# An fp32 transformer block on one Trainium2 core: its MLP by one level of Strassen's scheme

## The chip, the cores and the metric

The program runs on one core of a Trainium2 chip. The metric is the device time of one execution in microseconds, lower is better. The core's engines are called PE (TensorE, the matmul engine; its weight loads are PEld), DVE (VectorE), ACT (ScalarE), POOL (GpSimd) and SP (SyncE, which here only starts transfers). Each runs its own list of instructions in order; they meet through semaphores.

## The reference, cut to what matters

```python
for l in range(DEPTH):                      # DEPTH = 1
    h = _rmsnorm(x, ln_mix_g[l])
    ...                                     # projections, sparse attention, HGRN2, short conv
    x = x + mixed @ w_out[l]
    h = _rmsnorm(x, ln_mlp_g[l])            # x: 1024 tokens x 1024
    x = x + jnp.square(jax.nn.relu(h @ w_mlp_up[l])) @ w_mlp_down[l]   # 1024x4096, 4096x1024
...                                         # then a second block: MLA attention and pooling branch
```

All arrays are fp32. The MLP is two matrix products of 1024 x 1024 x 4096 multiply-adds each.

## The kernel before

Everything is kept transposed: a tile is 128 features (partitions) by 1024 tokens, and an activation of 1024 features is eight tiles `j`. To keep fp32 accuracy on PE, each operand is split in a high part (rounded to the engine's fp32r format) and a low part (the rest), and each product is three matmuls: high by high, high by low, low by high. A matmul has a 128x128 weight block and 512 tokens (`HALF`).

Matmul work is cut in **units**. A unit `n` makes one tile of 128 output features by 1024 tokens in one of two PSUM pairs, `pair[n % 2]`: two token halves by `kt` input tiles by three matmuls, so 48 matmuls where `kt` is 8. SP loads the weights of unit `n` to `raw` when POOL has split unit `n - 2`. POOL splits them in `w_hi` (L636, a cast) and `w_lo` (L638, a subtraction of two SBUF operands). PE multiplies (`product`, L708; `product_first`, L726, which takes the input tiles one by one as they become ready). The reader of the result frees the PSUM pair.

The stretch in question has, in order:

- the out product, 8 units. DVE adds each result to `xB` (L1893), squares it for the mean of squares (L1903), and ACT and DVE make the high and low parts of `xB * ln_mlp` in `actB` (L1411, L1905). The sum of squares is kept in `mt[1]` (L1908);
- the MLP, 4 groups of 16 units. The first 8 units of a group make 8 tiles of the hidden layer: DVE takes relu and multiplies by the root-mean-square factor `rstd` (L1922), ACT squares (L1418), DVE makes high and low part in `actA` (L1925, L1927). The other 8 units multiply these 8 tiles by their share of `w_mlp_down`, and DVE adds each result to `xB` (L1893). After the first MLP unit PE makes the mean of squares (key `ss1`, L981) from which ACT makes `rstd`. During the last 8 units the parts of the new `xB` are made for the second block (L1426, L1941);
- the second block's input product `in2`, 19 units.

The order on each engine is that of its code. The loops that are written with `units` are loops of the hardware, not unrolled. PE's whole inner loop is these lines:

```python
for half in halves:
    cols = slice(half * HALF, (half + 1) * HALF)
    for k in range(kt):
        wk = slice(k * P, (k + 1) * P)
        for i, (w, x) in enumerate(((w_hi, hi(k)), (w_hi, lo(k)), (w_lo, hi(k)))):
            last = nc.tensor.matmul(pair[par][:, cols], w[:, par, wk], x[:, cols], ...)
```

## Time and profile before

| | |
|---|---|
| time, median of 3 runs | 2575.23 us (2573.36 to 2575.47) |
| the profiled execution: its time, and its span | 2574.69 us, 2572.9 us |
| mean granted PE clock | 0.979 |
| busy: PE, DVE, POOL, ACT | 2445.7, 1281.0, 803.9, 558.5 us |
| moved to and from memory | 206.65 MB, mean 80 GB/s |

The span is what the profiler saw between the first and the last instruction; the device time has 1.8 us more. Matmuls overlap in the pipeline: a record's duration (389 ns) is longer than the distance to the next (about 227 ns), and the distance is what counts. Rows give a start and a duration in us, the engine, the line of the kernel, the operation, the tile that it writes and those that it reads; brackets hold the idle time before it and what ended it.

### The profile page before, as it was taken

To read this page: it belongs to the slowest core of one execution; us is meant where nothing else is said; L and a number is where in the kernel's file an instruction comes from. 1 tells how busy PE (TensorE), PEld (TensorE's weight loads), DVE (VectorE), ACT (ScalarE), POOL (GpSimd) and SP (SyncE) were. 2 spreads that over 40 slices of the span, in tenths; PEclk is the share of its full clock that TensorE was granted. 3 is DMA by queue.
4 is the path that set the end of the run, shared out by engine and by line. 5 is a ranking of instruction groups with operands and counts; after the bars stand their busy time and mean duration, and the time that the engine had idled before them with its cause. 6 is when DMAs were issued, how large, how long until landed. Compare 5 with 4: busy or idle time off the path is not lost. (4 is left out here: it accounts for less than half of the span.)

```text
span 2572.9 us, 30451 instructions
## 1 busy us (share of the span) xinstructions
PE 2445.7 (95%) x11722; PEld 2022.7 (79%) x11722; DVE 1281.0 (50%) x1639; ACT 558.5 (22%) x686; POOL 803.9 (31%) x741
## 2 busy tenths in 40 slices
PE   6999999989999899999999999999999999789996
PEld 4688878877888789787888888888888877579974
DVE  3699999975546245446541231321335200534378
ACT  3310241022222255211100000000000102334423
POOL 1123323322222364334333333333333331300154
PEclk9999999989999899999999999999999999999998
DMA  3022224642222421443111111111112110221122
GB/s 140 25 90 98 98 79 134 242 142 83 90 107 74 131 66 42 147 139 115 49 49 49 48 44 47 49 49 49 49 49 61 65 49 21 104 76 50 46 69 95
DMA packets 80036, 206.65 MB, mean 80 GB/s; under 512 B 7040, under 2 KB 30600, under 8 KB 79048
## 3 DMA queue, kind: packets, MB, share of 16 engines
q1 hardware_dynamic: 59552, 129.85, 16.0%
q10 hardware_dynamic: 20392, 75.52, 8.4%
q8 instruction: 64, 1.05, 0.2%
q14 instruction: 28, 0.23, 0.0%
HBM read 156.31 MB, written 50.34 MB: 80 GB/s over the span
## 5 line engine op out<-in xcount | busy, mean ns | idle before, releaser
L708 PE MATMUL pair<-actA,w_hi 128*128 128x512 f32 x3040 | 941.5, 391 | 0.0
L708 PEld LDWEIGHTS pair<-actA,w_hi 128*128 128x128 f32 x3040 | 568.8, 188 | 121.1 <-issue 4.8
L708 PE MATMUL pair<-actA,w_lo 128*128 128x512 f32 x1520 | 591.7, 389 | 0.0
L634 POOL TENSOR_TENSOR pad<-pad 128x1 f32<-128x1 f32 x206 | 49.8, 242 | 1636.7 <-PE pair L708 1293.2
L708 PE MATMUL pair<-actB,w_hi 128*128 128x512 f32 x1568 | 484.0, 390 | 0.0
L638 POOL TENSOR_TENSOR w_lo<-raw,w_hi 128x1024 fp32r<-128x1024 f32 (+2 forms) x206 | 475.3, 2307 | 16.5
L708 PEld LDWEIGHTS pair<-actB,w_hi 128*128 128x128 f32 x1568 | 294.4, 188 | 62.2 <-issue 1.4
L708 PEld LDWEIGHTS pair<-actA,w_lo 128*128 128x128 f32 x1520 | 285.3, 188 | 59.6
L708 PE MATMUL pair<-actB,w_lo 128*128 128x512 f32 x784 | 305.0, 389 | 0.0
L636 POOL CAST w_hi<-raw 128x1024 fp32r<-128x1024 f32 (+2 forms) x206 | 204.3, 992 | 0.0
L1893 DVE TENSOR_TENSOR xB<-pair,xB 128x1024 f32 (+1 forms) x40 | 49.0, 1225 | 297.8 <-PE pair L708 273.8
L1643 DVE MAX8 top<-pen 128x8 f32<-128x384 f32 (+5 forms) x192 | 171.7, 894 | 6.4
L708 PEld LDWEIGHTS pair<-actB,w_lo 128*128 128x128 f32 x784 | 147.2, 188 | 30.6
L1645 DVE MATCH_REPLACE8 pen<-top,pen 128x384 f32<-128x384 f32 (+5 forms) x192 | 168.1, 875 | 0.0
L1418 ACT ACTIVATE mt<-mt 128x1024 f32<-128x1024 f32 x32 | 34.0, 1061 | 563.4 <-DVE mt L1922 563.4
L1149 ACT ACTIVATE stage<-pair 128x1024 f32<-128x1024 f32 x52 | 53.3, 1025 | 397.1 <-PE pair L708 358.5
L1922 DVE SCALAR_TENSOR_TENSOR mt<-pair,rstd 128x1024 f32<-128x1024 f32 x32 | 39.2, 1225 | 185.9 <-PE pair L708 176.6
L708 PE MATMUL pair<-ysp,w_hi 128*128 128x512 f32 x336 | 103.3, 389 | 0.0
L1068 PE MATMUL pair<-actB,w_hi 128*128 128x512 f32 x256 | 83.0, 406 | 10.5 <-DVE xB L2079 6.7
L1685 DVE COPY_PREDICATED hattn<-hmask,pair 128x1024 f32<-128x1024 int32 x32 | 43.4, 1357 | 91.4 <-PE pair L813 91.4
L1817 DVE CUSTOM_DVE_ANT_0 Pr<-pair,pslot 128x128 f32<-128x128 f32 (+7 forms) x64 | 48.3, 757 | 75.8 <-PE pair L896 59.5
L726 PE MATMUL pair<-actA,w_hi 128*128 128x512 f32 x192 | 63.9, 416 | 16.3 <-DVE actA L1573 16.3
(285 smaller groups left out, 3068.9 us busy)
## 6 DMA issues: line engine op xcount, KB each, us to landing
raw<-w_in SPq DMA_DIRECT2D x80, 512.0 KB, 3.5
raw<-w_mlp SPq DMA_DIRECT2D x64, 512.0 KB, 3.5
proj<-stage ACTq DMA_DIRECT2D x52, 512.0 KB, 2.6
gates<-proj ACTq DMA_DIRECT2D x24, 512.0 KB, 5.4
raw<-w_out SPq DMA_DIRECT2D x24, 512.0 KB, 3.6
cin<-proj ACTq DMA_DIRECT2D x4, 1536.0 KB, 12.0
raw<-w_up SPq DMA_DIRECT2D x24, 256.0 KB, 2.7
X<-xT SPq DMA_DIRECT2D x8, 512.0 KB, 8.7
```

The lines of the kernel that those rows point to most:

```text
L634: nc.gpsimd.tensor_tensor(pad[:, 0:1], pad[:, 1:2], pad[:, 1:2], ALU.add)
L636: nc.gpsimd.tensor_copy(w_hi[:, par, 0:w], raw[:, par, 0:w]).then_inc(w_hi_ok, 1)
L638: nc.gpsimd.tensor_tensor(w_lo[:, par, 0:w], raw[:, par, 0:w], w_hi[:, par, 0:w].bitcast(F32), ALU.subtract).then_inc(w_split, 1)
L708: last = nc.tensor.matmul(pair[par][:, cols], w[:, par, wk], x[:, cols], start=(k == 0 and i == 0), stop=(k == kt - 1 and i == 2))
L726: last = nc.tensor.matmul(pair[par][:, cols], w[:, par, wk], x[:, cols], start=(k == 0 and i == 0), stop=(k == kt - 1 and i == 2))
L1068: mm = nc.tensor.matmul(pair[par][:, 0:HALF], w[:, par, wk], x[:, cols], start=(k == 0 and i == 0), stop=(k == NT - 1 and i == 2))
L1149: nc.scalar.activation(dst, pair[par][:, :], func).then_inc(unit_out[par], 1)
L1643: V.max(top8[:, :], sc).then_inc(topk, 1)
L1645: V.match_replace(sc, top8[:, :], sc, PICKED).then_inc(topk, 1)
L1685: V.copy_predicated(hattn[:, :, :], hmask[:, lv:lv + 1, :].broadcast_to([P, NB, P]), mpair(key)[:, :].rearrange("p (a b) -> p a b", b=P)). ...
L1817: V.tensor_tensor_reduce(Pr[i % 4][:, 0:n], s_out(i)[:, 0:n], pslot[:, i % 3, 0:n], -float(HD) ** -0.5, 3.0e38, ALU.add, ALU.min, low4[:, ...
L1893: V.tensor_tensor(x, pair[par][:, :], x, ALU.add).then_inc(unit_out[par], 1)
```

## The change

Both products of the MLP are made by one level of Strassen's scheme in Winograd's form. Features and tokens are cut in halves, so that a product of 2x2 by 2x2 blocks takes 7 block products `P1` to `P7` in place of 8. Their operands are blocks or sums of blocks, and their results are added up to the four result blocks.

- **Steps.** There are 32 steps (`STEPS`) of 7 products. In steps 0 to 15 (up) a step makes two tiles of the hidden layer: each product has 4 input tiles, 512 tokens, 3 matmuls, so 12 matmuls in one bank. In steps 16 to 31 (down) a step makes a quarter of the output from 4 hidden tiles: each product has 2 halves of a PSUM pair by 2 input tiles by 3, again 12 matmuls. All is unrolled.
- **Weights.** SP loads 1 MB for a step in `wraw`, double buffered. POOL makes the four sums of weight blocks (`weight_sum`); ACT makes the high part of each of the 7 weight operands (`weight_hi`, 128x512) and POOL the low part (128x512), into slots `wsp`: 5 slots to step 16, then 8, and 4 for the last step. A slot is written again when the product that used it is done.
- **Activations, up.** In the out product, whose units now go in the order `OUT_ORDER` (weights likewise), DVE also makes four sums of blocks from `xB` times `ln_mlp` (`chunk_sums`), in place in `xB`, which is parked in memory (`x_d`) before. ACT squares `xB` (DVE did), scales it (`scale_h`) and makes the high parts of the sums (`sum_hi`); DVE makes the low ones (`sum_lo`), 16 of each, 128x512.
- **Results, up.** DVE reads a bank after each product (`event`): a copy after P1, P5, P6, a sum after P2, P7, P3, and relu and `rstd` after P4. P6, P7, P4 go on in the bank of P1, and P3 in that of P5 (`banks`), so that each may begin when the reading of the product before it in that bank is done (`BANK_NEED`). Then `relu`, ACT's square (`square_out`), and four sums of hidden blocks on DVE (`unit_sums`). The seven hidden blocks are parked in memory (`hid_d`, 1.75 MB a step).
- **Down.** The parked blocks come back 512 KB at a time to `staged` (56 loads), ACT and DVE split them in the ring `tring` (`split_hi`, `split_lo`, 56 of each, 128x1024). `event` adds 128x1024 results to quarters of `xB`.
- **First step.** It has the order P1, P2, P5, P6, P3, P7, P4; `ss1` comes after P3; DVE's and ACT's work on the last tile, on the sums and on the results of this step is written out by hand.
- **Last step and `in2`.** The parts of `xB` are made in the last step and after it (`final_hi`, `final_lo`), and the first `in2` unit takes its input tiles in another order.

Core of the diff:

```diff
+OUT_ORDER = [0, 4, 1, 5, 2, 6, 3, 7]
+STEPS = 2 * N_PAIR
+WEIGHT = {"P1": "A11", "P2": "A12", "P3": "S4", "P4": "A22", "P5": "S1", "P6": "S2", "P7": "S3"}
+RAW_BLOCK = {"A11": 0, "A12": 1, "A21": 2, "A22": 3}
+RUN = [(0, p) for p in ("P1", "P2", "P5", "P6", "P3", "P7", "P4")]
+RUN += [(st, p) for st in range(1, STEPS) for p in ("P1", "P5", "P6", "P2", "P7", "P3", "P4")]
+NO = {key: i for i, key in enumerate(RUN)}
+N_RUN = len(RUN)
...
+def banks(i):
+    st, p = RUN[i]
+    kind = {"P2": "b", "P5": "c", "P3": "c"}.get(p, "a")
+    first, second = 1 - st % 2, st % 2
+    if st < N_PAIR:
+        return {"a": [(first, 0)], "b": [(first, 1)], "c": [(2 + st % 2, 0)]}[kind]
+    return {"a": [(first, 0), (first, 1)], "b": [(second, 0), (second, 1)],
+            "c": [(2 + st % 2, 0), (2 + st % 2, 1)]}[kind]
...
+        wsp = [at(f"wsp{i}", kb, [P, 2, HALF], F32R)
+               for i, kb in enumerate((168, 172, 176, 180, 16, 195.5, 199.5, 203.5))]
+        wsum = {"S1": at("wsum_a", 188, [P, HALF]), "S2": at("wsum_b", 190, [P, HALF]), "S4": at("wsum_c", 20, [P, HALF])}
+        wsum["S3"] = wsum["S1"]
...
+            def load_pair(st):
+                if st == 0:
+                    sp.wait_ge(w_split, FIRST["in2"])
+                elif st == 1:
+                    sp.wait_ge(unit_mm, FIRST["in2"])
+                else:
+                    sp.wait_ge(wt_ok, 7 * (st - 1))
+                sp.dma_start(wraw[:, st % 2, :], t["w_pair"][st]).then_inc(pair_in[st % 2], 16)
...
+            for i, (st, p) in enumerate(RUN):
+                if p == "P1":
+                    pool.wait_ge(pair_in[st % 2], 16 * (st // 2 + 1))
+                if i + 1 < N_RUN and WEIGHT[RUN[i + 1][1]][0] == "S":
+                    weight_sum(i + 1)
+                pool.wait_ge(wt_hi, i + 1)
+                k = RAW_BLOCK.get(WEIGHT[p])
+                src = wraw[:, st % 2, k * HALF:(k + 1) * HALF] if k is not None else wsum[WEIGHT[p]][:, :]
+                dst = wsp[W_SLOT[i]]
+                nc.gpsimd.tensor_tensor(dst[:, 1, :], src, dst[:, 0, :].bitcast(F32), ALU.subtract).then_inc(wt_ok, 1)
+            pool.wait_ge(wt_ok, N_RUN)
...
+            def run(i):
+                st, p = RUN[i]
+                pe.wait_ge(wt_ok, i + 1)
+                if BANK_NEED[i]:
+                    pe.wait_ge(evicted, BANK_NEED[i])
+                w = wsp[W_SLOT[i]]
+                fresh = p in ("P1", "P2", "P5")
+                if st < N_PAIR:
+                    subs, ks = 1, 4
+                    x = bsp[:, PARK_OF[p]] if PARK_OF[p] < 3 else tsp[:, PARK_OF[p] - 3]
+                else:
+                    subs, ks = 2, 2
+                    j = 7 * ((st - N_PAIR) // 2) + SPLIT_OF[p]
+                    pe.wait_ge(t_ok, 16 + j + 1)
+                    x = tring[j % T_RING]
+                for sub in range(subs):
+                    a, half = banks(i)[sub]
+                    out = pair[a][:, half * HALF:(half + 1) * HALF]
+                    for k in range(ks):
+                        if st == 0 and p in ("P1", "P2", "P3"):
+                            pe.wait_ge(lo_ok, base + NT + 2 * k + (1 if p == "P1" else 2))
+                        elif st == 0:
+                            pe.wait_ge(t_ok, 4 * (PARK_OF[p] - 3) + k + 1)
+                        wk = slice((sub * ks + k) * P, (sub * ks + k + 1) * P)
+                        for m, (wp, xp) in enumerate(((0, 0), (0, 1), (1, 0))):
+                            mm = nc.tensor.matmul(out, w[:, wp, wk], x[:, xp, k, :],
+                                                  start=(fresh and k == 0 and m == 0), stop=(k == ks - 1 and m == 2),
+                                                  skip_group_check=True)
+                mm.then_inc(mul_done, 1)
...
+            def weight_hi(i):
+                st, p = RUN[i]
+                if W_BEFORE[i] >= 0:
+                    act.wait_ge(mul_done, W_BEFORE[i] + 1)
+                elif W_SLOT[i] == 4:
+                    act.wait_ge(unit_mm, FIRST["in2"])
+                elif W_SLOT[i] > 4:
+                    act.wait_ge(squared_ok, 4 * N_PAIR)
+                k = RAW_BLOCK.get(WEIGHT[p])
+                if k is None:
+                    order = [q for q in RUN[7 * st:7 * st + 7] if WEIGHT[q[1]][0] == "S"]
+                    act.wait_ge(summed, 4 * st + order.index((st, p)) + 1)
+                    src = wsum[WEIGHT[p]][:, :]
+                else:
+                    act.wait_ge(pair_in[st % 2], 16 * (st // 2 + 1))
+                    src = wraw[:, st % 2, k * HALF:(k + 1) * HALF]
+                nc.scalar.copy(wsp[W_SLOT[i]][:, 0, :], src).then_inc(wt_hi, 1)
...
+            def scale_h(m):
+                j = OUT_ORDER[m]
+                act.wait_ge(x_tile[j], 32)
+                act.wait_ge(ss_sq, m + 1)
+                act.wait_ge(lo_ok, base + NT + m + 1)
+                nc.scalar.activation(xB[:, j, :], xB[:, j, :], ACT.Copy, scale=SM("ln_mlp", j)).then_inc(h_ok, 1)
...
+            def square_out(i):
+                st, p = RUN[i]
+                if p == "P4":
+                    act.wait_ge(evicted, i + 1)
+                else:
+                    act.wait_ge(relu_ok, 3 * st + ("P2", "P7", "P3").index(p) + 1)
+                if st == 0:
+                    act.wait_ge(t_ok, 12)
+                else:
+                    if p == "P2":
+                        act.wait_ge(b11_out, 16 * st)
+                    elif p != "P3":
+                        act.wait_ge(b2_out, 16 * st)
+                    act.wait_ge(tsum_ok, 16 + 4 * (st - 1) + {"P2": 1, "P3": 2, "P7": 4, "P4": 4}[p])
+                nc.scalar.activation(hid[:, HID_OF[p], :], u_of[p][:, :], ACT.Square).then_inc(squared_ok, 1)
...
+            def t_sums(src, dst, done, order):
+                b11, b12, b21, b22 = src
+                for q in order:
+                    if q == 0:
+                        V.tensor_tensor(dst[0], b12, b11, ALU.subtract).then_inc(tsum_ok, 1)
+                    elif q == 2:
+                        dve.wait_ge(tsum_ok, done + 1)
+                        V.tensor_tensor(dst[2], b22, b12, ALU.subtract).then_inc(tsum_ok, 1)
+                    elif q == 1:
+                        dve.wait_ge(tsum_ok, done + 2)
+                        V.tensor_tensor(dst[1], b22, dst[0], ALU.subtract).then_inc(tsum_ok, 1)
+                    else:
+                        dve.wait_ge(tsum_ok, done + 3)
+                        V.tensor_tensor(dst[3], b21, dst[1], ALU.subtract).then_inc(tsum_ok, 1)
...
+            def event(i):
+                st, p = RUN[i]
+                dve.wait_ge(mul_done, i + 1)
+                src = psum_of(i)
+                if st >= N_PAIR:
+                    if st == N_PAIR and p == "P1":
+                        dve.wait_ge(x_in, 16 * (NT + 1))
+                    if st == N_PAIR + 1 and p == "P1":
+                        dve.wait_ge(x_in, 16 * (NT + 3))
+                    first = {"P2": "P1", "P7": "P5", "P3": "P6"}.get(p)
+                    if first:
+                        dve.wait_ge(evicted, NO[st, first] + 1)
+                    acc = quarter(xB, st, {"P1": "P2", "P5": "P7", "P6": "P3"}.get(p, p))
+                    V.tensor_tensor(acc, src.rearrange("p (s n) -> p s n", n=HALF), acc, ALU.add).then_inc(evicted, 1)
+                    return
+                u = u_of[{"P1": "P2", "P5": "P7", "P6": "P3"}.get(p, p)][:, :]
+                used = {"P1": 1, "P5": 2, "P6": 3, "P4": 4}.get(p)
+                if used and st:
+                    dve.wait_ge(squared_ok, 4 * (st - 1) + used)
+                if p in ("P1", "P5", "P6"):
+                    V.tensor_copy(u, src).then_inc(evicted, 1)
+                elif p == "P4":
+                    V.scalar_tensor_tensor(u, src, 0.0, rstd[:, 0:HALF], ALU.max, ALU.mult).then_inc(evicted, 1)
...
+            def unit_sums(u):
+                dve.wait_ge(squared_ok, 4 * u + 4)
+                if u:
+                    dve.wait_ge(tsum_out, 16 * u)
+                t_sums([hid[:, HID_OF[p], :] for p in ("P2", "P3", "P4", "P7")],
+                       [hsum[:, q, :] for q in range(4)], 16 + 4 * u, (0, 2, 1, 3))
...
+            for m in range(NT - 1):
+                take_out(m)
+                low_out(m)
+                add_square(m)
+                dve.wait_ge(h_ok, m + 1)
+                chunk_sums(m // 2, (2, 1, 3) if m % 2 else (0,))
+            take_out(NT - 1)
+            for k in range(2):
+                sum_lo(0, k)
+            low_out(NT - 1)
+            for k in range(2, 4):
+                sum_lo(0, k)
+            event(0)
+            for k in range(3):
+                sum_lo(1, k)
+            add_square(NT - 1)
+            dve.wait_ge(ss_sum, NT + 1)
+            event(1)
+            event(2)
+            dve.wait_ge(h_ok, NT)
+            chunk_sums(3, (2, 1, 3))
+            sum_lo(1, 3)
+            event(3)
+            for k in range(4):
+                sum_lo(2, k)
...
+            for i in range(7, N_RUN):
+                st, p = RUN[i]
+                event(i)
+                if st < N_PAIR and p in ("P2", "P7", "P3"):
+                    relu(i)
+                if p == "P1" and st <= N_PAIR:
+                    unit_sums(st - 1)
+                for j in range(N_SPLIT):
+                    if T_TURN[j] == i:
+                        split_lo(j)
+                if st == STEPS - 1 and p in ("P5", "P6", "P2", "P7"):
+                    final_lo(STEPS - 2, ("P2", "P7", "P3", "P4")[("P5", "P6", "P2", "P7").index(p)])
+                if st == STEPS - 1 and p in ("P7", "P3", "P4"):
+                    final_lo(st, {"P7": "P2", "P3": "P7", "P4": "P3"}[p])
+            final_lo(STEPS - 1, "P4")
             base += NT
```

## Rows read from the trace of the kernel before

**Rows 1.** The page: busy time, share of the span and instructions of each engine.
```profile
PE 2445.7 (95%) x11722; PEld 2022.7 (79%) x11722; DVE 1281.0 (50%) x1639; ACT 558.5 (22%) x686; POOL 803.9 (31%) x741
```

**Rows 2.** Windows: the out product, and the MLP from its second unit on.
```profile
core 0: us, PE busy (x) PEld busy (x) DVE busy (x) ACT busy (x) POOL busy (x), PEclk, DMA share, GB/s
1184.00:1264.00 80.00, 80.00 (x355) 66.24 (x354) 49.36 (x29) 8.09 (x7) 32.29 (x21) 1.00 0.16 51
1276.30:1962.50 686.20, 686.20 (x3028) 568.19 (x3027) 185.44 (x134) 44.79 (x42) 223.88 (x189) 1.00 0.16 48
```

**Rows 3.** Timeline of DVE: sums that close the units of out and MLP.
```profile
1199.05 1.22 DVE L1893 TENSOR_TENSOR xB<-pair,xB 128x1024 f32<-128x1024 f32 x1 [3.93 <-PE pair L708]
1209.93 1.23 DVE L1893 TENSOR_TENSOR xB<-pair,xB 128x1024 f32<-128x1024 f32 x1 [3.92 <-PE pair L708]
...
1264.33 1.23 DVE L1893 TENSOR_TENSOR xB<-pair,xB 128x1024 f32<-128x1024 f32 x1 [3.92 <-PE pair L708]
...
1962.54 1.23 DVE L1893 TENSOR_TENSOR xB<-pair,xB 128x1024 f32 x1 [6.22 <-PE pair L708]
```

**Rows 4.** Timeline of PE at the end of the first MLP unit.
```profile
1272.97 0.62 PE L726 MATMUL pair<-actB,w_hi 128*128 128x512 f32 x2
...
1273.65 0.62 PE L726 MATMUL pair<-actB,w_hi 128*128 128x512 f32 x2
...
1275.01 1.88 PE L981 MATMUL pair<-mt,cst 128*128 128x512 f32 x4
1276.33 1.03 PE L708 MATMUL pair<-actB,w_hi 128*128 128x512 f32 x2
```

**Rows 5.** Groups by line and form on POOL, whole trace: count, busy us, mean ns.
```profile
L638 POOL TENSOR_TENSOR w_lo<-raw,w_hi 128x512 fp32r<-128x512 f32 x30 | 41.1, 1371 | 2.4
...
L671 POOL TENSOR_TENSOR ysp<-yin,ysp 128x512 fp32r<-128x512 f32 x16 | 20.4, 1275 | 1.3
```

**Rows 6.** The same groups on DVE, whole trace.
```profile
L1893 DVE TENSOR_TENSOR xB<-pair,xB 128x1024 f32 x32 | 39.2, 1225 | 268.0 <-PE pair L708 246.3 <-PE pair L726 21.6
...
L1673 DVE TENSOR_TENSOR hE<-hG 128x512 f32<-128x512 f32 x28 | 19.1, 683 | 0.0
...
L2079 DVE TENSOR_TENSOR xB<-pair,xB 128x512 f32<-128x512 f32 x12 | 8.3, 692 | 2.7 <-PE pair L1068 1.8
```

**Rows 7.** The same groups on ACT, whole trace.
```profile
L1522 ACT ACTIVATE sqh<-xB 128x512 f32<-128x512 f32 x16 | 10.1, 633 | 71.9 <-DVE xB L2079 46.0 <-DVE xB L2088 25.9
...
L1137 ACT CAST actA<-tmpn 128x1024 fp32r<-128x1024 f32 x8 | 8.4, 1046 | 10.1 <-DVE tmpn L1581 10.0
```

**Rows 8.** Timeline in the up-projections of the mixer, DVE beside POOL.
```profile
1113.79 1.23 DVE L1876 TENSOR_TENSOR prod<-pair,gates 128x1024 f32<-128x1024 f32 x1 [2.02 <-PE pair L708]
...
1114.66 1.28 POOL L638 TENSOR_TENSOR w_lo<-raw,w_hi 128x512 fp32r<-128x512 f32 x1
1115.05 1.98 DVE L1880 TENSOR_TENSOR mixed<-mixed,prod 128x1024 f32 x1
```

**Rows 9.** Timeline: DVE beside POOL in the out product, POOL alone in the MLP.
```profile
1189.43 1.23 DVE L1903 TENSOR_TENSOR mt<-xB 128x1024 f32<-128x1024 f32 x1
1189.47 3.44 POOL L638 TENSOR_TENSOR w_lo<-raw,w_hi 128x1024 fp32r<-128x1024 f32 x1
1190.62 3.37 DVE L1905 SCALAR_TENSOR_TENSOR actB<-xB,small,actB 128x1024 fp32r<-128x1024 f32 x1
...
1387.08 2.39 POOL L638 TENSOR_TENSOR w_lo<-raw,w_hi 128x1024 fp32r<-128x1024 f32 x1
```

**Rows 10.** PE after an idle stretch: the timeline's row, and that stretch's window.
```profile
1174.12 1.19 PE L726 MATMUL pair<-actA,w_hi 128*128 128x512 f32 x2 [5.96 <-DVE actA L1573]
```
```profile
1174.10:1180.20 6.10, 6.08 (x14) 4.77 (x15) 6.10 (x6) 4.28 (x5) 0.00 (x0) 0.50 1.00 394
```

**Rows 11.** DMA issues: queue, count, KB each, median us from issue to landing.
```profile
raw<-w_mlp SPq DMA_DIRECT2D x64, 512.0 KB, 3.5
...
cs_d<-cs ACTq DMA_DIRECT2D x1, 1024.0 KB, 4.8
```

403 lines of the change are left out of this document (319 added, 84 removed).

## The prediction

> **What bounds the kernel now.** I read the page's busy times first: PE 95% of the span, DVE 50%, POOL 31% [rows 1]. That says who to look at, not what a change is worth; for this I took the windows of the stretch that is changed. From the second MLP unit to the last, 686.2 us, PE is busy all the time at a granted clock of 1.00, DVE 185 us, POOL 224 us, ACT 45 us [rows 2]. The reader is to see there that nothing in the MLP waits for anything but PE. Next its pace. DVE's closing sums come every 10.88 us (1209.93 less 1199.05) [rows 3], and a unit has 48 matmuls: 0.2267 us for each. The same 0.68 us for three matmuls stands in a unit that waits for its input tiles one by one [rows 4], so a wait that is already met costs PE nothing. The MLP takes 1962.54 less 1264.33 = 698.2 us: 64 units by 10.88 = 696.3, and the rest is mainly `ss1`, 1276.33 less 1275.01 = 1.3 us [rows 3, 4].
>
> **What is removed.** 64 units by 48 are 3072 matmuls; 32 steps by 7 by 12 are 2688. 384 fewer, of the same shape and order (high by high, high by low, low by high), by 0.2267 us: **-87.0 us**. A step of 84 matmuls is then 19.04 us, a product 2.72 us. These two are the budgets of all that follows. Nothing in the diff makes a single matmul cheaper or dearer.
>
> **What is added, and the port.** Prices for 128x512: a POOL subtraction of two SBUF operands 1.28 us (1275 ns; in a more disturbed stretch 1371) [rows 5]; a DVE operation 0.69, from PSUM or SBUF; a DVE operation on 128x1024 1.23 [rows 6]; ACT 0.63, and 1.05 for 1024 [rows 7]. What DVE and POOL do to each other matters more than these. A DVE product of a PSUM and an SBUF operand from 1113.79 to 1115.02 lies across a POOL subtraction that starts at 1114.66, and both keep their time (1.23, 1.28). The next DVE sum, of two SBUF operands, starts at 1115.05 and takes 1.98: it waits for POOL's end at 1115.94, then needs 1.09 [rows 8]. The other way round, POOL starting 0.04 us after a DVE operation of two SBUF operands takes 3.44 where one alone takes 2.39, and the DVE operation after it 3.37 [rows 9]. So two operations with two SBUF operands each exclude each other, and PSUM readers are free. That is what the Trainium skill says (SBUF — State Buffer, "Who interferes with whom": one shared read port, held for the whole instruction). A POOL operation thus delays DVE by up to 1.28 us, and a DVE one of 128x512 that was waiting delays POOL by about 0.55 us (0.69 less the 0.14 that [rows 8] show to be saved after a wait).
>
> *Up step, POOL.* 4 sums and 7 low parts: 11 x 1.28 = 14.1, gaps of 0.08 (between the records) 0.9, and 7 DVE operations with two SBUF operands (3 relu, 4 sums) x 0.55 = 3.9: 18.9 us of 19.04. It just fits. *Down step, POOL.* The same 15.0 and 3.5 `split_lo` x 1.09 = 3.8: 18.8. *ACT.* 7 x 0.63 and 4 x 0.63 (up) or 3.5 x 1.05 (down): 7 to 8 us. *DVE.* Up 14 x 0.69 = 9.7 and about 0.6 of waiting on 7 of them, 13.9; down 7 x 1.23 + 3.5 x 1.9 = 15.3. No engine but PE exceeds 19.04, so none of it adds to the sum as long as the weights are ahead: with 5 slots a weight has 4 products, 10.9 us, from the end of the product that frees its slot.
>
> *Up step, DVE in order.* P6, P7, P4 and P3 need that the bank was read one product earlier, so a reading has 2.72 us less what DVE is busy with. The tight place is behind P1. P1 ends at 2.7 us of the step; ACT then makes one weight part and the square of the last step's P4, to 4.3; `unit_sums`, four sums of which each waits for the one before, meets one or two POOL operations, to 8.7; then the readings of P5 and P6, to 10.2; PE wants P7 at 10.88. Slack 0.7 us; with POOL in front of all four sums it would be 4 x 1.9, to 11.9, readings to 13.3, and PE waits 2.4 us. After its free weights are made POOL waits for slots, and its gaps lie where the four sums do, so I take the small end: 0.3 us a step, **+4.5** for 15 steps, bounds 0 and 36. *Down.* A reading of 1.23 and, every second product, a `split_lo` of 1.9: 4.4 of 5.44 us. I take 0.2 a step, **+3.2**, bounds 0 and 16.
>
> *Transfers.* Up, 1 MB of weights in and 1.75 MB out a step; down, 1 MB and 3.5 x 0.5 MB in: 2.75 MB in 19.04 us, about 145 GB/s. 512 KB land in 3.5 us, 1 MB in 4.8 [rows 11]; all are asked for more than half a step ahead of need, so nothing. Were a load of weights a full step late, POOL and then PE would wait for it, 5 us each time. In SP's list the load for step `u + 2` stands behind the store of the sums of `u - 1`; that store is let go at about 8.7 us, the load at the same time, and it is needed 19 us later. Of the hand-over from up to down the narrowest is `xB`: sums of step 15 made at 9 us of step 16, stored by 14, 2 MB of `xB` back by 23 to 25, wanted at 21.8 and through P6 of step 17 at 24.5. **+2**, bounds 0 and 6.
>
> **The first step** is where I expect to lose most. Before, the low part of the last tile was wanted at the end of a unit and nothing waited. Now, from the end of the last out unit (0): ACT stands in its list behind the high part for P6, whose sum POOL reaches only after two sums and two low parts, about 2.6 us; the last tile's high part is ready at 5.0, its low part at 7. DVE has, before P6 can finish, 15 operations in a row: `xB` sum, the last low part, `add_square` (1.23 each), and 12 of 0.69, 12.0 us and 0.7 of gaps, with 2.6 at the start for ACT and some 5 of POOL's in between: about 20. P6 ends near 21; without waits it would have ended at 10.9. Loss 10. Then between P6 and P4 DVE has three readings and 8 `sum_lo`, 11 x 0.74 = 8.1 and 3 of POOL's, where PE has P3, `ss1` and P7, 6.7: loss 4.5. Here P7 and P4 stand next to each other in one bank. PE will be idle for some us twice. After 5.96 us of idle time PE began at 1174.12 with the clock at 0.50, to about 1180 [rows 10]: the lower of two levels, 1.2 GHz for 2.4, and half of 5 to 6 us is lost, 2.6. I count it once, less what overlaps: **+16**, bounds 5 (POOL never in the way, ACT in time) and 28. The Trainium skill (TensorE: Matmul & The Clock Gate, "Part 1: The HAM clock gate") says the same, that idle PE goes to half clock; the row gives the price.
>
> *Last step.* In it DVE has 7 readings and 7 `final_lo`, about 22 us of work for 19; the first `in2` unit takes the late tiles last, 5.4 us and 8.2 us after it starts. **+1**, bounds 0 and 4.
>
> **Sum.** -87.0 + 16 + 4.5 + 3.2 + 2 + 1 = -60.3. Against the profiled execution, 2574.7 (span 2572.9 + 1.8), that is 2514.4; the median of the runs is 0.5 above that execution. I say **2514 us**.
>
> **Unrolling.** The MLP was in hardware loops and now is a list of 2688 matmuls. The Trainium skill (Runtime: NRT & Kernel Launch, "Instruction fetch mechanics") calls a taken branch dear and sequential fetching hidden. The trace gives the branches no price: 64 units take 64 x 10.88, loops or not. So no gain from this.
>
> **Rivals.**
> *A, the readings are late.* DVE meets POOL at each of the four `unit_sums`, and in the down steps a `split_lo` pushes a reading past its product. PE waits 1 to 2 us a step, 31 steps: +31 to +62 in place of 7.7, 2537 to 2568. For it: slack of 0.7 us, and POOL at 18.9 of 19.04. Against it: a PE that waits gives POOL room.
> *B, the weights are late, and it is slower.* POOL becomes the engine that sets the step. Place: `wt_ok` ahead of each product. Without waits and gaps its time is 11 operations; a step is 11 x t + 0.9 + 3.9, and all is lost when it reaches 19.04 + (87.0 - 19)/32 = 21.2, that is t = 1.49 us. At 1.6 it is 22.4, 32 x 3.4 = 108 more less 87 and plus 19: 2614. For it: the 1371 ns of [rows 5] where DVE is near, which include waits. Against: 1275 where it is not.
> *C, the first step is cheap.* ACT and DVE are in time but for one or two us, all the rest hidden: -87 + 8 = 2496.
> *D, the change does less than it counts.* Each product starts late by what a fresh bank and a check of two semaphores cost: 224 x 0.2 = 45, 2551 with the rest small. Against: [rows 4], six matmuls behind each wait at full pace.
>
> **How the numbers follow.** Forecast 0.60, its own range 2499 to 2529 (the first step's bounds, and half of A's lower end). A 0.15, B 0.07, C 0.09, D 0.05, anything else 0.04. The range goes from 2495 (C) to 2552 (half of A, D), which leaves out the other half of A, B and part of the rest, about 0.18. Two runs of this kernel differ by less than 0.1%, so 0.2%, 5 us, is what a measurement can tell from none. Faster: the forecast, C, D, A but for its very end, half of the rest, 0.90; the same 0.03; slower: B and part of the rest, 0.07.
>
> **What would show it.** The steps: in windows of the new up and down stages PE busy all the time at 1.00, a step 19.1 to 19.4 us; 20 or more in the up steps with PE waiting for DVE's reading ahead of P7 is A; PE waiting for POOL is B. The port: relu and `unit_sums` with means well over 0.69, the readings from PSUM at 0.69. First step: 33 to 37 us from the end of the out units to the first product of step 1, PE waiting in P6 for a low part by DVE, the clock once at 0.50. If that stretch takes 22 us it is C. Pace: three matmuls in 0.68 us across product borders; more is D. The forecast is wrong if the time lies above 2529 or below 2499.

## The result

The changed kernel takes 2510.28 us (median of 4 runs, 2506.73 to 2513.70), the one before 2574.36 (median of 4, 2573.36 to 2575.47): a ratio of 0.9752, 95% interval 0.974 to 0.9764, 64 us less. The forecast was 2514. The profiled execution took 2511.02 us, its span is 2509.2 at a mean granted clock of 0.977; the span before was 2572.9. The runs of the changed kernel lie 0.28% apart, those of before 0.08%. The 0.1% that the prediction gave as the difference between two runs holds for neither kernel: where the kernel before ran nine times on one chip, beside the experiments, its runs spread by 0.18 to 0.41% (2569.89 to 2580.45 at the widest). The last section says what goes with that scatter.

The page of after, in answer to [rows 1]: busy time of each engine, share of the span, instructions.

```profile
PE 2364.3 (94%) x11338; PEld 1952.3 (78%) x11338; DVE 1541.5 (61%) x1927; ACT 772.1 (31%) x1029; POOL 1100.7 (44%) x901
```

PE's busy time falls by 81 us, and DVE, ACT and POOL take on 260, 214 and 297 us. That those 771 us cost little has to be read by stages. Windows of 20 us of after, in answer to [rows 2]: steps 0 and 1, an up step, the hand-over from up to down, a down step.

```profile
1264.00:1284.00 20.00, 15.31 (x60) 11.84 (x59) 17.80 (x20) 11.65 (x19) 8.63 (x7) 0.91 0.24 79
1304.00:1324.00 20.00, 17.12 (x69) 13.64 (x68) 12.78 (x14) 5.86 (x10) 17.63 (x13) 0.91 0.35 119
1364.00:1384.00 20.00, 20.00 (x90) 16.57 (x89) 13.61 (x16) 6.49 (x11) 17.07 (x12) 1.00 0.42 145
1584.00:1604.00 20.00, 13.98 (x53) 10.56 (x52) 19.86 (x15) 10.76 (x16) 19.53 (x11) 0.92 0.52 200
1764.00:1784.00 20.00, 20.00 (x90) 16.57 (x89) 15.70 (x12) 8.19 (x12) 17.16 (x12) 1.00 0.36 132
```

The columns are those of [rows 2]: PE, PEld, DVE, ACT, POOL, then clock, DMA share, GB/s. In the steady steps PE is busy for 20.00 of 20.00 us at clock 1.00, with POOL at 17.1. All that is lost is lost in two places, the first 50 us and the hand-over, where DVE is busy for 19.86 of 20. PE's own rows there, from its timeline, with the idle time before each and what ended it:

```profile
1271.91 0.96 PE L1226 MATMUL pair<-bsp,wsp 128*128 128x512 f32 x3 [2.18 <-DVE bsp L2296]
...
1281.75 0.96 PE L1226 MATMUL pair<-tsp,wsp 128*128 128x512 f32 x3 [2.51 <-DVE tsp L2281]
...
1291.32 3.02 PE L1226 MATMUL pair<-tsp,wsp 128*128 128x512 f32 x12 [1.38 <-POOL wsp L899]
...
1300.96 3.00 PE L1226 MATMUL pair<-tsp,wsp 128*128 128x512 f32 x12 [1.18 <-DVE u_c L2329]
...
1309.57 4.53 PE L1226 MATMUL pair<-tsp,wsp 128*128 128x512 f32 x12 [2.88 <-DVE u_c L2329]
...
1589.63 2.96 PE L1226 MATMUL pair<-tring,wsp 128*128 128x512 f32 x12 [0.74 <-DVE tring L2354]
...
1600.88 9.29 PE L1226 MATMUL pair<-tring,wsp 128*128 128x512 f32 x33 [4.93 <-DVE tring L2354]
```

In order these are the last chunk of P2 and of P6 in step 0, its P4, then P6 and P7 in step 1, and P5 and P2 of step 16. Twelve matmuls that take 4.53 us instead of 2.9 are partly at the lower clock. Apart from 0.35 us at 1592.95 and 0.52 at 1624.97, PE waits for nothing else from the first step to `in2`.

The account of the stretch, from the last sum of the out product (DVE L2254 at 1265.01) to PE's first matmul of `in2` (1899.77), 634.8 us: 32 steps of 19.04 are 609.3, `ss1` 1.3, and the rest 24.2 is lost. Read from one reading of P4 to the next, step 0 takes 29.44 after the out product (9.1 lost), step 1 25.20 (6.2), steps 2 to 14 exactly 19.04 each, the hand-over (steps 15 to 17) loses 9.1, the other down steps nothing. Of the 9.1 of the hand-over 6.5 are waits (0.74, 0.35, 4.93 and 0.52), and most of the rest is the lower clock behind the long one: 33 matmuls take 9.29 us there where 7.6 would be full pace. Before, the stretch took 698.2 [rows 3].

| us lost | forecast | measured |
|---|---|---|
| first step | 16 | 9.1 |
| the other 15 up steps | 4.5 | 6.2, all of it in step 1 |
| hand-over and transfers | 2 | 9.1 |
| down steps | 3.2 | 0 |
| last step | 1 | 0 |
| sum | 26.7 | 24.4 (24.2 by the whole stretch) |

So the sum came out right although none of its terms did: 11.1 us too many in three of them stand against 8.8 too few in two. The experiments ask whether the first term (-87.0) is what it was taken for, why the steady steps lose nothing, and what sets the two losses.

### The profile page after: what moved, and what is told of

Its sections match the earlier page's. It is cut to its first block and busy times, and to the rows that moved or that the text cites. A ratio compares the mean times of both kernels' runs of the same rounds, so it can differ in the third digit from the quotient of the medians.

```text
span 2509.2 us, 30514 instructions
## 1 busy us (share of the span) xinstructions
PE 2364.3 (94%) x11338; PEld 1952.3 (78%) x11338; DVE 1541.5 (61%) x1927; ACT 772.1 (31%) x1029; POOL 1100.7 (44%) x901
## 5 line engine op out<-in xcount | busy, mean ns | idle before, releaser
L935 PE MATMUL pair<-actA,w_hi 128*128 128x512 f32 x2144 | 666.7, 392 | 0.0
L815 POOL TENSOR_TENSOR pad<-pad 128x1 f32<-128x1 f32 x142 | 38.9, 274 | 1165.5 <-PE pair L935 857.2
L935 PEld LDWEIGHTS pair<-actA,w_hi 128*128 128x128 f32 x2144 | 400.8, 188 | 86.7 <-issue 5.3
L935 PE MATMUL pair<-actA,w_lo 128*128 128x512 f32 x1072 | 417.4, 389 | 0.0
L819 POOL TENSOR_TENSOR w_lo<-raw,w_hi 128x1024 fp32r<-128x1024 f32 (+2 forms) x142 | 316.6, 2230 | 11.4
L1226 PE MATMUL pair<-tring,wsp 128*128 128x512 f32 x1344 | 307.4, 391 | 6.5 <-DVE tring L2354 5.7
L1226 PEld LDWEIGHTS pair<-tring,wsp 128*128 128x128 f32 x1344 | 253.1, 189 | 60.7 <-issue 7.4
L1226 PE MATMUL pair<-tsp,wsp 128*128 128x512 f32 x768 | 186.3, 395 | 8.0 <-DVE u_c L2329 4.1
L935 PE MATMUL pair<-actB,w_hi 128*128 128x512 f32 x576 | 178.1, 390 | 0.0
L1226 PEld LDWEIGHTS pair<-bsp,wsp 128*128 128x128 f32 x576 | 108.3, 188 | 25.2 <-DVE bsp L2296 2.6
L935 PEld LDWEIGHTS pair<-actB,w_hi 128*128 128x128 f32 x576 | 108.1, 188 | 23.3 <-issue 1.0
L935 PE MATMUL pair<-actB,w_lo 128*128 128x512 f32 x288 | 112.1, 389 | 0.0
```

The source lines that it names most:

```text
L815: nc.gpsimd.tensor_tensor(pad[:, 0:1], pad[:, 1:2], pad[:, 1:2], ALU.add)
L819: nc.gpsimd.tensor_tensor(w_lo[:, par, 0:w], raw[:, par, 0:w], w_hi[:, par, 0:w].bitcast(F32), ALU.subtract).then_inc(w_split, 1)
L1226: mm = nc.tensor.matmul(out, w[:, wp, wk], x[:, xp, k, :], start=(fresh and k == 0 and m == 0), stop=(k == ks - 1 and m == 2), skip_group_ ...
```

## The experiments

The tables below give, beside the medians, stretches of the profiled execution: steps without a wait repeat there to 0.1 us, while the runs of one kernel lie 3 to 13 us apart. Each ratio is to the kernel before on the same chip (its medians are 2571.79 to 2573.68).

**What the matmuls alone are worth.** The kernel before, with seven of eight input tiles in each MLP unit: 384 fewer matmuls and no scheme around them. It leaves out an eighth of both MLP products.

```diff
-                    product_first(n0, 8, hB, lB, lo_ok, base + NT)
+                    product_first(n0, 7, hB, lB, lo_ok, base + NT)
```
(and the same in the three other calls)

> The kernel before, with 7 of 8 input tiles in each MLP unit (the eighth is left out of all 64 units): 384 matmuls fewer and nothing added. If PE's pace alone sets the MLP: 384 x 0.2267 = 87.0 us less, 2487 us. If part of the pace comes from what ends each unit (reading, weight split), the gain is smaller, 40 to 80 us.

Measured 2487.08 (2483.43 to 2491.28) against 2571.79, ratio 0.9662 [0.9643, 0.968]: -84.7 by the medians, and -87 by the ratio's centre. The term holds, and what the scheme costs in total is 2510 less 2487, 23 us, as the account above has it.

**Why the steady steps lose nothing: POOL's room.** Two kernels in which two or four of a step's seven low parts are computed twice.

```diff
+                if st and p in ("P1", "P2"):          # four: "P1", "P5", "P2", "P4"
+                    nc.gpsimd.tensor_tensor(dst[:, 1, :], src, dst[:, 0, :].bitcast(F32), ALU.subtract).then_inc(pool_step, 1)
+                    again += 1
+                    pool.wait_ge(pool_step, again)
                 nc.gpsimd.tensor_tensor(dst[:, 1, :], src, ...
```

> POOL makes the low parts of P1's and P2's weights twice in steps 1 to 31, 13 operations a step for 11. By the prediction's sum (18.9 us of POOL a step, each more 1.36): 21.6 us a step, +2.6 x 31 = 80, about 2590 us. If POOL really has the 2.8 us of idle time a step that the trace shows (16.3 busy of 19.04, waits for the port in it): 19.0 to 19.7, 0 to 20 us more, 2510 to 2531 us.

> The same for P1, P5, P2 and P4: 15 operations a step. By the prediction's sum 18.9 + 5.4 = 24.3, +5.3 x 31 = 164, about 2674 us. By the trace's busy time 16.3 + 4 x 1.5 = 22.3, +3.3 x 31 = 101, about 2611 us. In both PE waits for POOL in every step.

Measured: two more, 2544.14 (2539.53 to 2547.26), ratio 0.989 [0.9868, 0.9912]; four more, 2618.08 (2614.96 to 2621.47), ratio 1.018 [1.0161, 1.02]. An up step takes 19.90 us with two more; with four they alternate between 24.9 and 19.7. Windows, first with two more, then with four:

```profile
1400.00:1420.00 20.00, 19.40 (x86) 15.78 (x85) 13.66 (x14) 6.48 (x11) 19.12 (x14) 1.00 0.43 150
```

```profile
1380.00:1400.00 20.00, 16.95 (x68) 13.90 (x69) 11.92 (x15) 5.86 (x10) 18.82 (x14) 0.91 0.40 145
1400.00:1420.00 20.00, 19.63 (x87) 15.97 (x86) 11.06 (x13) 6.37 (x11) 19.69 (x15) 1.00 0.35 120
```

In the changed kernel POOL is busy for 17.07 of 20 us, 16.12 a step by windows of one step, where the prediction had 18.0 and 0.9 of gaps. Two more operations of 1.28 make 18.7, which would still fit in 19.04; yet the step is 19.90, with POOL busy for 19.0 of it, and the kernel takes 34 us more, where this theory had 0 to 20. So the step grows before POOL is full. With four more the sum of busy times is 21.2, the steps are 22.3 on average, and 2618 us is near the 2611 of that theory. The prediction's own sum is well off in both (2590 and 2674). With two more the way is the prediction's A, not B: PE's wait in each step is for a reading by DVE.

```profile
1414.94 2.98 PE L1231 MATMUL pair<-tsp,wsp 128*128 128x512 f32 x12 [0.60 <-DVE u_c L2334]
```

With four more I had expected a wait for POOL in every step. In the up steps PE's waits are again all for DVE's readings (up to 4.1 us, where POOL is busy for 96% of the time); in the down steps POOL is busy for 99%, and the trace names no releaser. DVE shows why in the up steps. First, on ACT, a high part that waits for POOL and the square behind it, and on DVE the four differences, which need this square; then the differences and the readings behind them in the changed kernel's steady step:

```profile
1373.68 0.62 ACT L1695 CAST wsp<-wsum_c 128x512 fp32r<-128x512 f32 x1 [2.71 <-POOL wsum_c L886]
1374.21 0.63 ACT L1762 ACTIVATE hid<-u_c 128x512 f32<-128x512 f32 x1
1374.87 1.79 DVE L2268 TENSOR_TENSOR hsum<-hid 128x512 f32<-128x512 f32 x1 [3.30 <-ACT hid L1762]
1376.69 1.66 DVE L2271 TENSOR_TENSOR hsum<-hid 128x512 f32<-128x512 f32 x1
1378.39 1.65 DVE L2274 TENSOR_TENSOR hsum<-hid,hsum 128x512 f32<-128x512 f32 x1
1380.07 1.63 DVE L2277 TENSOR_TENSOR hsum<-hid,hsum 128x512 f32<-128x512 f32 x1
```

```profile
1341.41 0.69 DVE L2329 COPY u_c<-pair 128x512 f32<-128x512 f32 x1 [2.03 <-PE pair L1226]
1342.60 1.35 DVE L2263 TENSOR_TENSOR hsum<-hid 128x512 f32<-128x512 f32 x1 [0.49 <-ACT hid L1757]
1343.99 0.69 DVE L2266 TENSOR_TENSOR hsum<-hid 128x512 f32<-128x512 f32 x1
1344.71 0.69 DVE L2269 TENSOR_TENSOR hsum<-hid,hsum 128x512 f32<-128x512 f32 x1
1345.44 1.66 DVE L2272 TENSOR_TENSOR hsum<-hid,hsum 128x512 f32<-128x512 f32 x1
1347.02 1.27 DVE L2329 COPY u_c<-pair 128x512 f32<-128x512 f32 x2
```

A difference of two SBUF operands takes 0.69 us where POOL pauses and 1.65 where POOL runs without a gap; a reading from PSUM takes 0.69 in both. In the steady step POOL waits for a slot just when two of the four run. So the gaps in POOL's list are what keeps DVE in time: fill them, and DVE's readings are late. With four more there is a second way: the square stands in ACT's list behind the high part of a sum of weights, POOL makes that sum late, and DVE waits 3.30 us before the differences, where it waits 0.49 in the changed kernel. How much of the loss each way makes isn't separated.

**The order of step 0.** The changed kernel with all products in plain order (P1, P5, P6, P2, P7, P3, P4) in step 0 too.

```diff
-RUN = [(0, p) for p in ("P1", "P2", "P5", "P6", "P3", "P7", "P4")]
-RUN += [(st, p) for st in range(1, STEPS) ...
+RUN = [(st, p) for st in range(STEPS) ...
```

> The first step in the order of all others (P1, P5, P6, P2, P7, P3, P4), ss1 still behind P3. If the reordering is worth what it lets PE do while DVE makes sum_lo: P6 is then wanted 2.7 us earlier with the same low parts, and P4 waits for the factor and its weight behind it: step 0 is 4 to 8 us longer, 2514 to 2518 us. If DVE's list alone sets the end of the first step, nothing: within 2 us of 2510.

Measured 2520.5 (2518.19 to 2523.03), ratio 0.9793 [0.9778, 0.9808]: 10 us more than with the reordering. Step 0 takes 38.26 us and step 1 22.56, together 6.2 more than in the changed kernel's profile, which is within the 4 to 8 expected. PE's longest waits there are 3.73 us for DVE's low part in P6 and 4.14 us for POOL's weight of P4. The rest of this profile's difference isn't the reordering's: the stages behind the last reading of step 31, whose instructions are the same, take 614.45 us in this profile and 608.08 in the changed kernel's, with PE busy 6.4 us longer for as many matmuls. First the changed kernel, then this one:

```profile
1901.12:2509.20 608.08, 555.52 (x2747) 455.29 (x2745) 263.66 (x367) 172.33 (x210) 168.75 (x148) 0.97 0.20 65
1906.75:2521.20 614.45, 561.89 (x2747) 458.92 (x2745) 264.31 (x367) 172.26 (x210) 166.61 (x148) 0.96 0.20 64
```

That is the granted clock again, and it varies between runs of one program, as the last section says. The reordering earns its place by some 6 us.

**Differences spread over the step.** The four differences of each unit one at a time, behind the readings of P1, P5, P6 and P2, splits ahead of them: first in all steps, then in the up steps only.

```diff
-                if p == "P1" and st <= N_PAIR:
-                    unit_sums(st - 1)
                 for j in range(N_SPLIT):
                     if T_TURN[j] == i:
                         split_lo(j)
+                if p in ("P1", "P5", "P6", "P2") and st <= N_PAIR:    # then: st < N_PAIR, and all four together as before in step 16
+                    unit_sum(st - 1, {"P1": 0, "P5": 2, "P6": 1, "P2": 3}[p])
```

> The four hidden sums of an up step are made one behind each of the readings of P1, P5, P6 and P2 instead of all behind P1, and behind a split_lo due there. If DVE's order at the hand-over (8.4 us lost in step 16) and in step 1 (6.2 us) is the cause: 6 to 10 us less, 2500 to 2504 us, steps 2 to 14 unchanged at 19.04. If POOL or the transfers are the cause: within 2 us of 2510.

> The change, with the four differences of each middle unit taken apart in the up steps 1 to 15 only (one behind each reading of P1, P5, P6 and P2), and left together where the down-projection begins. If the 6.2 us that step 1 loses are the readings of P5 and P6 waiting behind four differences in a row, step 1 falls from 25.2 to about 20.4 us, as in the run that spread all of them, and nothing is given back at the hand-over: 4.8 us less than the changed kernel, about 2505.5. If the spreading itself makes the hand-over late, whatever is done there, the time stays at 2510 or goes to 2515 to 2521.

Measured 2521.25 (2518.06 to 2522.84), ratio 0.9798 [0.9781, 0.9814], for all steps; 2508.36 (2507.24 to 2510.18), ratio 0.975 [0.9737, 0.9764], for the up steps, where the changed kernel, run beside it, had 2512.10 (2511.64 to 2514.39), 0.9765 [0.9751, 0.9778]. In both, step 1 falls from 25.2 to 20.41 us, 4.8 less, as the second expectation said: its loss is the four differences ahead of P5's and P6's readings. The first expectation, 6 to 10 us less with all of them spread, failed: that kernel is 9 to 11 us slower. Spread in step 16 too, the differences cost more there than they save in step 1, since the last one is made much later. SP's rows at the hand-over, of the changed kernel and then of the one that spreads all: store of the differences (L735), and weights of step 18 (L724), between which stands the reload of the residual.

```profile
1598.56 0.37 SPq L735 DMA_DIRECT2D hid_d<-hsum  x1
1606.28 0.45 SPq L724 DMA_DIRECT2D wraw<-w_pair  x1
```

```profile
1607.49 0.37 SPq L735 DMA_DIRECT2D hid_d<-hsum  x1
1615.60 0.45 SPq L724 DMA_DIRECT2D wraw<-w_pair  x1
```

The two traces have different zeros: counted from the reading of P4 in step 14, the store goes out at 31.4 us in the changed kernel and at 42.8 in the other. Everything behind the store moves with it. PE waits 3.75 us ahead of P4 of step 16 for the reading of P7, which stands behind the last difference; 1.24 us in step 17 for a reading that waits 4.52 us for the reload; and 6.53 us ahead of P7 of step 17, by the weights of step 18, in the way that the next experiments show.

**The hand-over.** In the changed kernel DVE makes the split that P2 of step 16 waits for (the last row here) behind the four differences:

```profile
1592.77 0.68 DVE L2263 TENSOR_TENSOR hsum<-hid 128x512 f32<-128x512 f32 x1
1593.48 1.69 DVE L2266 TENSOR_TENSOR hsum<-hid 128x512 f32<-128x512 f32 x1
1595.21 1.65 DVE L2269 TENSOR_TENSOR hsum<-hid,hsum 128x512 f32<-128x512 f32 x1
1596.90 1.64 DVE L2272 TENSOR_TENSOR hsum<-hid,hsum 128x512 f32<-128x512 f32 x1
1598.46 2.28 DVE L2354 TENSOR_TENSOR tring<-staged,tring 128x1024 fp32r<-128x1024 f32 x1
```

Four kernels change what DVE does there. One puts the split for P2 of step 16 ahead of all four differences; one puts it between the second and the third (in the kernel that spreads them in the up steps); one moves all splits of parked blocks one product earlier, so that four of them lie ahead (in the kernel of the next paragraph); the last leaves the four differences of the last unit out, so that the parked ones are those of the unit before.

```diff
+                for j in range(N_SPLIT): ...          # split first
                 if p == "P1" and st <= N_PAIR:
                     unit_sums(st - 1)
-                for j in range(N_SPLIT): ...
```
```diff
-        turn.append(... if turn else r + 2)            # splits one product earlier
+        turn.append(... if turn else r + 1)
```
```diff
-                if p == "P1" and st <= N_PAIR:         # last differences left out
+                if p == "P1" and st < N_PAIR:
                     unit_sums(st - 1)
-                sp.wait_ge(tsum_ok, 4 * (u + 5))
+                sp.wait_ge(tsum_ok, 4 * (min(u, N_PAIR - 2) + 5))
```

> Only the place of a split_lo changes: at the hand-over it is made ahead of the four sums, not behind them. P2 of step 16 then doesn't wait 4.9 us, but the readings of P5 and P6 still stand behind the sums, so P7 waits in its place: 0 to 3 us less, 2507 to 2510 us. If the late operand of P2 is all: 5 to 6 us less.

> The run before this one, with the split for product P2 of step 16 put between the second and the third of the last unit's four differences. If two chains share the 9 us of the hand-over (the split that P2 waits for, and the store of the differences, the reload of the residual and the first reading of step 17), P2's wait of 4.9 us falls by some 3.3 and the store goes out 2.3 us later, which the reading in step 17 passes on in part: 0 to 3 us less than the run before. If the chain of the store alone sets the hand-over, the time is 2 us more; if the split alone did, 3.3 less.

> The run with the three moves in step 0 and the spread differences, and the splits of the read-back middle blocks one product earlier each (the first in step 15's P2 instead of P7), so that four and not three of them lie ahead of the last unit's differences, the first in the 2.2 us in which VectorE is idle in step 15. If the order of splits and differences on VectorE sets the hand-over, P2 of step 16 no longer waits (4.9 us), P7 waits some 2 us in its place, and the differences and their store go out when they did: 2 to 3 us less than without it, a hand-over of 6 to 7 us, and some 2505 for the kernel. If VectorE's load is what bounds the hand-over, the differences start later by what was put ahead of them and the reading in step 17 passes it on: 0 to 1 less or more, some 2508.

> The changed kernel with the four differences of the last middle unit left out (its parked differences are those of the unit before; all waits are otherwise as they were, and the store goes out as soon as the last square is parked). If these four differences, 5.7 us of VectorE between the first reading of step 16 and the split that P2 needs, are the cause of what the hand-over loses, 9.1 us fall to 1 to 4: 5 to 8 us less than the changed kernel, 2503 to 2507. If the transfers (the store, the reload of 2 MB, the next weights) set it whatever VectorE does, the store still leaves earlier by 5.7 us, but the wait moves to the weights of step 18 or the parked blocks, and less than 3 us are gained.

The column of the stretch is from the start of the reading of P4 in step 14 to that of the last product of step 31; it holds nothing of steps 0 and 1.

| kernel | stretch, us | PE waits longest for | median, us (range) | ratio |
|---|---|---|---|---|
| changed kernel, second time | 334.0 | split for P2, 4.97 | 2512.10 (2511.64 to 2514.39) | 0.9765 |
| spread in up steps | 334.2 | the same, 4.94 | 2508.36 (2507.24 to 2510.18) | 0.9750 |
| split first | 338.2 | reading of P6 in step 16, 5.57 | 2517.47 (2511.45 to 2520.25) | 0.9774 |
| split in the middle | 336.7 | the same, 3.76 | 2512.94 (2511.16 to 2517.00) | 0.9770 |
| splits earlier | 338.4 | the same, 5.86 | 2513.86 (2508.48 to 2521.64) | 0.9777 |
| differences spread there too | 347.5 | reading of P6 in step 17, 6.53 | 2521.25 (2518.06 to 2522.84) | 0.9798 |
| last differences left out | 330.6 | split for P3, 2.22 | 2513.01 (2506.53 to 2516.63) | 0.9764 |

My expectation of a gain was wrong for the three that move splits: 2.5 to 4.2 us are lost against the same kernel without that edit (334.0, 334.2, and 334.4 with the three moves below). The kernel with the split first shows two reasons. Its rows, of PE, DVE and ACT:

```profile
1608.53 21.06 PE L1226 MATMUL pair<-tring,wsp 128*128 128x512 f32 x84 [5.57 <-DVE xB L2322]
1631.87 23.43 PE L1226 MATMUL pair<-tring,wsp 128*128 128x512 f32 x95 [2.29 <-POOL wsp L899]
1607.21 1.21 DVE L2322 TENSOR_TENSOR xB<-pair,xB 128x1024 f32<-128x1024 f32 x1
1627.50 2.00 DVE L2354 TENSOR_TENSOR tring<-staged,tring 128x1024 fp32r<-128x1024 f32 x1 [4.81 <-ACT tring L1762]
1625.89 0.62 ACT L1690 CAST wsp<-wraw 128x512 fp32r<-128x512 f32 x1 [9.24 <-DMA wraw<-w_pair]
```

The first is DVE's list, and not the reload, for which no reading waits here. P7 of step 16 needs that P6's result was read, and that reading (1607.21) stands behind the splits and the differences in whatever order they are made. Counted from the reading of P4 in step 14 it ends at 37.0 us in the changed kernel, with the split first and with the split in the middle alike (38.9 with the splits earlier). So P2 starts 5.1 us sooner with the split first, and P7 then waits in its place: it starts at 37.1 us for 38.1, but now runs itself at the lower clock that P2 had, so that P3 starts at 41.7 for 40.8. The second is the store, which is made 1.9 to 2.2 us later in all three. It moves the weights of step 18; ACT's high part of them (1625.89) waits for their landing, and in ACT's list the high part of a block stands behind it; DVE's split (1627.50) waits for that, and the reading of P6 of step 17 stands behind the split. P7 of step 17 then waits 2.29 us, for 0.52 in the changed kernel. The trace puts this wait down to POOL, but P7's weight was made before POOL's own 7.87 us of waiting for the weights of step 18, and the reading of P6 ends 0.1 us before P7 starts.

Without the differences 3.4 of the 9.1 us are gone, less than the 5 to 8 expected of them as the whole cause and a little more than the 3 of the transfers' theory. The store goes out with the last square, 7.4 us earlier, and the next wait is for P3's split, which DVE can't begin; from its timeline:

```profile
1598.84 1.21 DVE L2322 TENSOR_TENSOR xB<-pair,xB 128x1024 f32<-128x1024 f32 x1
1604.26 1.88 DVE L2354 TENSOR_TENSOR tring<-staged,tring 128x1024 fp32r<-128x1024 f32 x1 [4.21 <-ACT tring L1762]
```

and ACT's, where the high part of a sum of weights comes first, and POOL made that sum only at 1602.56:

```profile
1602.65 0.62 ACT L1690 CAST wsp<-wsum_b 128x512 fp32r<-128x512 f32 x1 [1.88 <-POOL wsum_b L874]
1603.18 1.04 ACT L1762 CAST tring<-staged 128x1024 fp32r<-128x1024 f32 x1
```

So the hand-over is bound from three sides that lie within a few us: DVE's list up to the reading of P6, the chain of store, reload and next weights, and POOL's sums of weights, the last two through ACT's order. Taking one away gives less than its length. The first two were moved by experiments; POOL's part is read from rows, since no run took work from POOL there. The median of this last kernel doesn't show its 3.4 us. Its profiled execution lost more in steps 0 and 1 (31.04 and 26.43 us, for 29.45 and 25.19 in the changed kernel run again) and behind step 31 (614.4 us for 608.0), which is the clock's part, below.

**Three moves in step 0**, on top of the spread in the up steps: the low part of the last residual tile ahead of two splits of sums, the last weight ahead of the root on ACT, the three relus ahead of P4's reading.

```diff
             take_out(NT - 1)
+            low_out(NT - 1)
             for k in range(2):
                 sum_lo(0, k)
-            low_out(NT - 1)
...
+            for p in ("P2", "P7", "P3"):
+                relu(NO[0, p])
             event(6)
-            for p in ("P2", "P7", "P3"):
-                relu(NO[0, p])
...
+            weight_hi(6)
             wait_ready(act, "ss1")
```

> The run with the differences spread in the up steps only, with three moves in step 0: the low part of the last residual tile ahead of two splits of sums (P2 waits 2.2 us for it), the weight of the last product ahead of the root (the product waits 1.4 us for it), and the three scalings by 1/rms ahead of the reading of the last product, in the 3.8 us that VectorE is idle there (the first products of step 1 wait 1.2 us behind them). If each of these waits is set by the order alone, 2 to 4.5 us less than the run with the spread, about 2502. If the high and low parts of the sums bound step 0 as a whole, so that a wait only moves on, 0 to 1 less, about 2505.

> The changed kernel once more, as the measure for the other three on the same chip: 2507 to 2514 us, with 9.1 us lost in step 0, 6.2 in step 1 and 9.1 at the hand-over.

Measured 2508.00 (2504.03 to 2514.07), ratio 0.9756 [0.9739, 0.9773]. By the stretch from the last sum of the out product to the last reading of step 31: 636.2 us in the changed kernel run again, 633.2 with the spread, 631.7 with the three moves. The 1.2 us in step 1 are gone, P2's 2.2 went and 0.8 ahead of P5 and 0.7 in P6 came in its place, and P4's 1.4 became 1.2; but P6's last wait grew from 2.5 to 4.09. Its last three matmuls start 16.9 us after the last sum of the out product, for 16.7 in both other kernels: the work on DVE ahead of them sets that moment, and a wait removed before it comes back there. The kernel with the split in the middle shows the same with step 0 unchanged: there the 21 matmuls behind P2's wait took 4.98 us and not 6.54, and P6 then waited 4.08 us and began at the same 16.7. So what PE gains ahead of that moment, by order or by clock, is lost in that wait. The kernel's span, 2502.1, is the lowest of all, yet its runs spread from 2504 to 2514, and the medians don't tell it from the spread alone; the 2502 that I expected was not reached. It beats the changed kernel by 4.5 us in its own stretch; that the whole kernel is faster isn't shown.

## Why the prediction was right, and where it was not

- **The removed matmuls, -87.0.** Right: 84.7 to 87 by the cut kernel, and steps of exactly 19.04 us.
- **Up steps, +4.5.** Steps 2 to 14 lose nothing; step 1 loses 6.2, for a reason of its own (below). For the steady ones the working was close (DVE's reading of P6 ends 9.8 us after the step's start, for 10.2 forecast), but a slack of 0.7 to 1.1 us that repeats exactly costs nothing, and I charged 0.3 a step for it. POOL's price was too high: 18.9 us with gaps, measured 16.1 busy. I let each of seven DVE operations cost POOL 0.55; rows show five of its eleven operations lengthened by some 0.45.
- **Down steps, +3.2, and last step, +1.** The same error: both 0. `in2` starts without a wait.
- **First step, +16.** Too high: 9.1 (waits of 2.2 in P2, 2.5 in P6 and 1.4 in P4, and some 3 of slower matmuls, most of it half clock). The first product of step 1 came 29 us after the out units, not 33 to 37. P6 ended at 17.5 us, not near 21: of the operations that I put in front of it in a row, those from 1275.86 on met no POOL operation, since POOL stood idle for 8.26 us there, and those of 128x512 took 0.69. P4 waited 1.4 us for its weight, where 4.5 were forecast.
- **Step 1** has no term of its own. It lost 6.2. It is the case that the prediction worked out for P7 and then set aside: POOL, behind with its weights, has no gap, all four differences take 1.64 to 1.71, and PE waited 2.88 us for the 2.4 worked out, then lost some 1.5 to the lower clock; before that P6 waited 1.18 us behind the three relus of step 0.
- **Hand-over, +2, bounds 0 to 6.** This failed: 9.1, above its bounds. I had timed only the chain of the residual, from differences that end 9 us into step 16. They began at 6.8 us and not at 4.3, since splits stand in front, and ended at 12.5; even so that chain was met, and no reading waited for the reload. What was left out: the split for P2 stands behind those differences on DVE, which from 1583.24 on is busy without a pause. PE waited 4.93 us for it, and some 1.5 went to the lower clock behind that wait. Nor was that split alone: the reading of P6, which P7 needs, stands in the same list, and with the split moved ahead PE waited 5.57 us for it. The splits there meet POOL and take up to 2.31 us where 1.9 was forecast.
- **Rivals.** A didn't happen, and with two more POOL operations it did, at 0.9 us a step: its mechanism is real, its condition wasn't met. B's point was about right: slower than before was forecast from a step of 21.2, and four more POOL operations, with steps of 22.3 on average (24.9 and 19.7 in turn), end 1.8% slower; but B's sign, PE waiting for POOL, isn't seen in the up steps even there. C fell (steps 0 and 1 lost 15.3). D fell: no product border costs anything in 27 steps.
- **Unrolling** showed no gain, nor loss: 0.2267 us a matmul with or without the hardware loops.

In sum 6.9 us too many for the first step and 4.2 for the down steps and the last offset 1.7 too few for the up steps and 7.1 at the hand-over. The removed matmuls make the direction and most of the size; that the forecast came within 4 us of 2510 is luck.

## What to carry to other kernels

When work moves from PE to other engines, first make sure of the steady step: compare each engine's busy time to the step, and if no reading is late by these sums, charge nothing for small slack, since the up steps here repeat to 0.01 us. Put the care in the borders, where two stages' work meets on one engine: list there everything that stands in front of the first operation that each product needs, not only the longest chain of transfers. An engine with idle time may be needed idle: POOL's pauses kept two of DVE's four differences at 0.69 us, and two more operations in them cost 34 of the 64 us that the change had won.
